# Two projections behind each layer norm computed from the stream before it is normalised

## The reference

```
x = layer_norm(ALPHA * x + mod[2] * y, ln1_g, ln1_b)          # y: the token mixer's output projection
f = conv_ffn(modulate(x, mod[3], mod[4]), w_up, ...)          # modulate(x, shift, scale) = layer_norm(x) * (1 + scale) + shift
x = layer_norm(ALPHA * x + mod[5] * f, ln2_g, ln2_b)
h = modulate(x, next_mod[0], next_mod[1]);  next_in = h @ w_in
```

## Time and profile before

| | us |
|---|---|
| median of 3 runs | 3637.96 |
| lowest and highest | 3637.43, 3638.48 |
| the profiled execution | 3641.97 |
| its span | 3639.8 |
| PE busy | 3432.4 |
| DVE busy | 1618.0 |
| POOL busy | 1076.3 |
| ACT busy | 1004.5 |

### The profile page before, as it was taken

One profiled execution on the slowest core, in us unless ns is written; L12 is line 12 of the kernel. 1 busy time (PEld: TensorE's weight loads), 2 busy tenths in 40 slices (PEclk: granted clock), 3 DMA queues, 4 the chain that ended last, 5 costly groups with the idle time before them and its releaser, 6 DMA issues.

```text
span 3639.8 us, 57152 instructions
## 1 busy us (share of the span) xinstructions
PE 3432.4 (94%) x24613; PEld 2827.6 (78%) x24613; DVE 1618.0 (44%) x2601; ACT 1004.5 (28%) x1438; POOL 1076.3 (30%) x412
## 2 busy tenths in 40 slices
PE   6999999979989999999999899999979899999998
PEld 5777778867768888888886677788867678888887
DVE  4333563056166334334334533463086564434436
ACT  4334564124132111111112333464133221111111
POOL 1212101302333333333333212201312444444443
PEclk9999999999999999999999999999989999999999
DMA  5111001352201111111112111000162111111111
GB/s 182 37 27 30 1 2 50 97 187 58 66 24 35 39 37 35 37 39 36 41 35 76 23 24 27 24 2 24 35 193 76 52 41 52 46 47 47 52 47 64
DMA packets 269678, 186.41 MB, mean 51 GB/s; under 512 B 45405, under 2 KB 249077, under 8 KB 269429
## 3 DMA queue, kind: packets, MB, share of 16 engines
q1 hardware_dynamic: 268272, 182.28, 16.7%
q10 hardware_dynamic: 1156, 0.48, 0.1%
HBM read 174.33 MB, written 8.39 MB: 50 GB/s over the span
## 4 chain that ended last, share of the span: by engine, by line
PE 83%; DVE 9%; issue 3%; ACT 2%; POOL 1%; DMA 1%; ACTq 0%; POOLq 0%; DVEq 0%; PEldq 0%
PE psum L1032 60%; PE psum L891 6%; PE psum L1132 5%; PE psum L1282 3%; PE psum L900 2%; PE psum L1210 2%; DVE f_t L2281 1%; PE psum L1058 1%; DVE y_chan L2172 1%; DVE c_x L2136 1%; PE psum L960 1%; PE psum L1241 1%; DVE h_lo L1931 1%; ACT f_t L2816 1%; PE psum L1366 1%
## 5 line engine op out<-in xcount | busy, mean ns | idle before, releaser
L1032 PE MATMUL psum<-h_hi,w_split 128*128 128x512 f32 (+1 forms) x5952 | 1437.7, 370 | 18.3 <-POOL w_split L846 8.1
L844 POOL TENSOR_SCALAR w_split<-w_raw 128x1024 fp32r<-128x1024 f32 x196 | 552.0, 2816 | 2390.4 <-PE psum L1032 1653.1
L1032 PEld LDWEIGHTS psum<-h_hi,w_split 128*128 128x128 f32 x5952 | 1030.3, 188 | 223.7 <-issue 12.0
L1032 PE MATMUL psum<-h_lo,w_split 128*128 128x512 f32 (+1 forms) x2976 | 799.9, 368 | 0.0
L1032 PEld LDWEIGHTS psum<-h_lo,w_split 128*128 128x128 f32 x2976 | 516.0, 188 | 97.6
L2281 DVE SCALAR_TENSOR_TENSOR f_t<-psum,vec,f_t 128x1023 f32<-128x1023 f32 (+1 forms) x264 | 260.2, 1013 | 705.4 <-ACT f_t L2816 702.3
L846 POOL TENSOR_TENSOR w_split<-w_raw,w_split 128x1024 fp32r<-128x1024 f32 x196 | 477.0, 2434 | 16.4
L1032 PE MATMUL psum<-f_hi,w_split 128*128 128x512 f32 (+1 forms) x1696 | 416.9, 371 | 15.7 <-DVE y_chan L2172 10.7
L2816 ACT ACTIVATE f_t<-psum,vec 128x1280 f32<-128x1280 f32 (+1 forms) x88 | 115.4, 1311 | 910.2 <-PE psum L1032 886.7
L1032 PEld LDWEIGHTS psum<-f_hi,w_split 128*128 128x128 f32 x1696 | 295.9, 188 | 80.3 <-issue 25.0
L2172 DVE SCALAR_TENSOR_TENSOR y_chan<-psum,mods,y_chan 128x1024 f32<-128x1024 f32 (+1 forms) x256 | 247.2, 1003 | 172.2 <-PE psum L1032 171.8
(11 more groups left out here) (275 smaller groups left out, 3471.6 us busy)
## 6 DMA issues: line engine op xcount, KB each, us to landing
w_raw<-in_w_up_dram SPq DMA_DIRECT2D x88, 512.0 KB, 3.8
ada_late<-in_w_ada_dram SPq DMA_DIRECT2D x32, 1024.0 KB, 7.3
w_raw<-in_w_down_dram SPq DMA_DIRECT2D x44, 512.0 KB, 3.8
w_raw<-in_w_in_dram SPq DMA_DIRECT2D x42, 512.0 KB, 3.9
ada<-in_w_ada_dram SPq DMA_DIRECT2D x4, 2048.0 KB, 17.9
ada_early<-in_w_ada_dram SPq DMA_DIRECT2D x8, 1024.0 KB, 5.3
x_first<-in_x_dram SPq DMA_DIRECT2D x8, 512.0 KB, 12.6
o_x<-in_x_dram SPq DMA_DIRECT2D x8, 512.0 KB, 3.9
```

Of the source, the lines that this page charges most:

```text
L844: pool.tensor_scalar(w_hi[:, n % 2], w_raw[:, n % 2], 1.0, None, ALU.mult).then_inc(s["w_hi_done"], 1)
L1032: last = pe.matmul(columns(key, t0, t0 + tn), weight, a[:, k, t0:t0 + tn], start=(k == order[0] and j == 0), stop=(k == order[-1] and j == 2))
```

## The change

For each stage, the two projections behind it no longer wait for the normalised halves.

- **Halves of the raw stream.** ACT writes `h_hi` = `y_chan` times the channel factor `ln_a` (`raw_high`), DVE writes the remainder to `h_lo` (`raw_low`). This happens as the channel tiles of the stream come, for stages 0 and 2 beside the last output projection. The two projections (`raw_gemms`) take these halves.
- **The tail within them.** The last statistics, the turning of the sums and a product of the small set-up rows with the raw, unsplit weights (`shift_products`, 16 matmuls of fp32) are issued between the steps `k` of the first projection. The spreading of the token factor and of the token rows, and the first corrections, are issued between those of the second. The spreading uses banks 6 and 7, piece by piece, and no accumulator slot.
- **Closing.** Three matmuls for each accumulator (`close`) add token rows times the shift vectors, behind step 3 of the second projection and at its end. DVE then multiplies the accumulator by the token factor: in place in phase F (`scaled`), on the way out in phase A (`raw_part`, which takes ACT's copies of `a_k` and `a_vt`).
- **The normed halves** are made afterwards into the same `h_hi`, `h_lo`, each `k` once the second raw projection has used it (`z_used`). The next projections, `up` 1 0 and `up` 1 1 with the second two steps behind, or `a_q` alone, run as they come.
- **DVE, ACT and POOL** get the work of FFN tile 0 (`scaled`, `conv`, `begin`, `silu`) between the steps of the normed halves, and POOL the splitting of the next weights between its products. The four residuals of the first pair stand together behind tile 1. The moments are spread within `up` 2 0.
- **Loads.** The weight loads that would overwrite the raw tiles' buffers wait for `raw_shift`.
- The barriers of all engines behind phases O and F of these stages become plain signals.

```diff
@@ load_weights
                     sp.wait_ge(s["w_ready"], n - 1)
+                    for st, raw in enumerate(RAW_TILES):
+                        if plan.tiles[n - 2] in raw:
+                            sp.wait_ge(s["raw_shift"], st + 1)
@@ POOL
-                pool.wait_ge(*freed("bc", st, 0))
-                for k in range(1, KT, 2):
+                pool.wait_ge(s["bc_taken"], done + many)
+                for n, k in enumerate(range(1, KT, 2)):
                     if k >= 3:
                         pool.wait_ge(s["hk_ready"], KT * st + k - 1)
-                    pool.tensor_tensor(kt_[:, 1, 0:w], y_chan[:, k, 0:w], r_b[:, 0:w], ALU.mult).then_inc(s["kt_ready"], 1)
+                    pool.tensor_tensor(kt_[:, 1, 0:w], y_chan[:, k, 0:w], r_of(st)[:, 0:w], ALU.mult).then_inc(s["kt_ready"], 1)
+                    if n < len(tiles):
+                        split_up_to(*tiles[n])
...
-                odd_products(2 * l)
+                odd_products(2 * l, [("up", l, 1, half) for half in range(2)])
@@ PE, raw_gemms
+                def shift_products():
+
+                    wait((s["set_widened"], st + 1))
+                    wait((s["set_taken"], 2 * st + 2))
+                    wait((s["var_ready"], 2 * st + 1))
...
+                        for k in range(KT):
+                            last = pe.matmul(psum[64 * t:64 * t + 56, 6, 3 * P:4 * P], set_wide[:, k, :], weight[:, k],
+                                             start=(k == 0), stop=(k == KT - 1))
+                    last.then_inc(s["raw_shift"], 1)
...
+                def close(t):
+                    wait((s["raw_shift_taken"], st + 1))
+                    wait((s["bc_taken"], done + 2 * many))
+                    for t0, tn, who in pieces(q_tiles(l)):
+                        rows_ = slice(64 * t + 32 * who, 64 * t + 32 * who + 24)
+                        last = pe.matmul(slot(*keys[t])[:, t0:t0 + tn], raw_vec[rows_, :], ranks_of(st)[rows_, t0:t0 + tn],
+                                         start=False, stop=True)
+                    fill(last, *keys[t])
...
+                gemm(tiles[0], keys[0], parts, ready=lambda k: (s["z_ready"], KT * st + k + 1),
+                     between={2: last_sums, 4: lambda: sum_columns(st), 6: shift_products}, fills=False, closes=False)
+                between = {n: spread_two(2 * n) for n in range(many)}
+                between.update({3: corrections(0, (0, 1)), 4: close_first, 5: corrections(1, (0, 1)), 6: corrections(1, (2,))})
+                gemm(tiles[1], keys[1], parts, between=between, used=s["z_used"], fills=False, closes=False)
+                close(1)
@@ PE, phase_a
-                    norm_tail(2 * l - 1)
-                    normed_gemms(2 * l - 1, [("in", l, COL["a_" + name]) for name in "kv"], [("A", l, r, name) for name in "kv"])
+                    raw_gemms(2 * l - 1, lambda: leave(pe, full("Y", l - 1, NPAIR - 1, KT - 1), "F", l - 1))
+                    normed_gemms(2 * l - 1, [("in", l, COL["a_q"])], [("A", l, r, "q")], groups(l), 0)
@@ PE, phase_f
-                normed_gemms(2 * l, [("up", l, 0, half) for half in range(2)], [("F", l, 0, half) for half in range(2)])
-                spread_moments(l)
+                raw_gemms(2 * l, lambda: leave(pe, full("W", l, KT - 1), "O", l))
+                normed_gemms(2 * l, [("up", l, 1, half) for half in range(2)], [("F", l, 1, half) for half in range(2)],
+                             groups(l), 2)
@@ DVE
+            def raw_low(st, k):
+
+                dve.wait_ge(s["z_hi"], KT * st + k + 1)
+                for a, b, who in [(0, LAT, 0)] + [(LAT, T, 1)] * (q_tiles(STAGES[st][0]) == NT):
+                    ins = dve.scalar_tensor_tensor(out=h_lo[:, k, a:b], in0=y_chan[:, k, a:b], scalar=ln_a[:, k, who:who + 1],
+                                                   in1=h_hi[:, k, a:b].bitcast(F32), op0=ALU.mult, op1=ALU.subtract)
...
+                normed_tiles(2 * l, {0: [partial(scaled, 0)], 1: [partial(conv, 0, 0), partial(scaled, 1)],
+                                     2: [partial(conv, 0, 1)]})
...
+                        for half in range(2):
+                            conv(f + 1, half)
+                        gated(f + 1)
+                        for k in range(4):
+                            residual(k)
```

More of the change, by code:

```diff
@@ L1012, in spread_gates, with gemm @@
                     last.then_inc(s["x1b_full"], 1)
-            def gemm(tile, key, parts, kt=KT, col=0, x_hi=h_hi, x_lo=h_lo, ready=None, between={}, order=None, fills=True):
+            def gemm(tile, key, parts, kt=KT, col=0, x_hi=h_hi, x_lo=h_lo, ready=None, between={}, order=None, fills=True,
+                     used=None, closes=True):
                 n = plan.tile[tile]
@@ new lines, in to @@
+                def to(part, many):
+                    return colmat[:, 0:n].rearrange("p c (r j) -> p c r j", j=32)[:, :, :, part:part + many]
+                dve.wait_ge(s["dve_step"], own.n)
+                for part in (0, 4):
+                    also(dve.tensor_copy(to(part, 3), four(high.bitcast(F32), 3)))
+                step(dve.tensor_tensor(to(8, 3), four(whole, 3), four(high.bitcast(F32), 3), ALU.subtract))
+                step(dve.tensor_copy(raw_high, raw))
+                for part in (12, 16):
+                    also(dve.tensor_copy(to(part, 4), four(raw_high.bitcast(F32), 4)))
@@ L2214, in phase_o @@
                     key = ("W", l, m)
+                    if m == KT - 1:
+                        for k in range(5):
+                            raw_low(2 * l, k)
                     dve.wait_ge(*full(*key))
@@ L2229, in phase_o @@
                         undo_residual(m + 2)
+                    if m == 2:
+                        widen_setup(2 * l)
+                for k in range(5, KT):
+                    last = raw_low(2 * l, k)
                 return last
@@ L2288, in conv, with scaled @@
                                 also(ins)
-                w = T if ctx_too else LAT
+                def scaled(half):
+                    acc = slot("F", l, 0, half)[:, 0:w]
+                    dve.wait_ge(*full("F", l, 0, half))
+                    say("scaled", dve.tensor_tensor(acc, acc, r_of(2 * l)[:, 0:w], ALU.mult))
                 def gated(f):
@@ L2516, in norm_tail, with raw_high @@
                         act.wait_ge(*corr_taken(st, k, piece))
+                    act.wait_ge(s["z_used"], KT * st + k + 1)
                     say("hk_hi", copy(h_hi[:, k, 0:w], kt_[:, k % 2, 0:w]))
+                    for work in behind.get(k, ()):
+                        work()
+            def raw_high(st, k, key):
+                l, which = STAGES[st]
+                act.wait_ge(s["set_built"], 2 * st + 2)
+                act.wait_ge(*freed(*key))
+                if not which and k < KT - 1:
+                    act.wait_ge(s["o_used"], (KT - 1) * l + k + 1)
+                for a, b, who in [(0, LAT, 0)] + [(LAT, T, 1)] * (q_tiles(l) == NT):
+                    ins = act.activation(h_hi[:, k, a:b], y_chan[:, k, a:b], ACT.Identity,
+                                         scale=ln_a[:, k, who:who + 1], bias=zeros[:, 0:1])
+                    if b == P * q_tiles(l):
+                        say("z_hi", ins)
+                    else:
+                        own.on(ins)
             def squares(st, m, key):
```

364 lines of the change are left out of this document (245 added, 119 removed).

## The result

The changed kernel takes 3648.77 us (median of 7 runs, 3644.38 to 3656.3), the kernel before 3637.96 (7 runs): a ratio of 1.0029, with a 95% interval of 1.0018 to 1.0039. So it is 10.8 us slower (6.5 to 14 by the interval), where 2.2 us less was forecast. The time lies just inside the stated range, whose upper end (3649) was set for the rival of the late start. The profiled execution took 3647.04, span 3645.2.

What follows compares the result with a forecast made beforehand. PE, busy 3432.4 of 3639.8 us, was taken as the bound, so only its waits or slow work could be won. Stage 0 +3.2, stage 2 +5.4, stage 1 -6.4: 2.2 us won, 3638.0 to 3635.8, range 3621 to 3649.

Steps and rivals of the forecast that it cites:

- the rival of the late start: Costlier fp32 matmuls and DVE's tail start the second raw projection 5 to 6 us later: 13.5 lost, 3651, chance 0.18.
- stage 0: First changed stage: fourth down projection at 1160.6 instead of 1163.8, a gain of 3.2 us.
- stage 1: Bias loads issued behind the eighth low half, 11.8 us later, delay the first scores: 6.4 us lost, 1.7 of it clock.
- stage 2: Like stage 0 with 1024 tokens: fourth down projection at 2976.1 instead of 2981.5, a gain of 5.4 us.
- the late residuals: DVE waits until 12 us into `up` 2 0, then does four residuals; PE waits 1.4 at `up` 3 0, 0.9 later.
- the widening: Widening of sets on DVE, taken to cost nothing beside projections; 1.5 us a stage if that cover is gone.
- PE's raw part: First raw projection with statistics, turning and 16 fp32 matmuls (4.0 us): 21.5 us in stages 0 and 1, 17.3 in stage 2.
- B: Time in each stage when the last output or down projection ends and the last statistics start, before the change; 998.7 in stage 0.
- Stage 0's chain: DVE, POOL and ACT make normed halves in turn; eighth low half at T + 58 = 1078.2, DVE the bound.
- T: Start of the second raw projection, forecast at B + 21.5 in stages 0 and 1, about B + 17.3 in stage 2.
- The rival of a quick chain: Pairs of normed halves take 9.4 us in all stages, fp32 matmuls 2.0: 13 won, 3625, chance 0.27.
- The clock rival: PE stays at 1.2 GHz in the normed steps, costing stages 0 and 2 2 to 3 us each: 3641, chance 0.12.

Runs made afterwards that it cites:

- bias_early: Changed kernel, with SP issuing the 16 bias loads behind stage 1's fourth low half instead of its eighth: 3641.78 us, 1.0005 of the kernel before.
- before_bias_early: Kernel before the change, with the same earlier issue of the bias loads: 1.0006 of the kernel before.
- widen_later: Changed kernel, with stage 1's widening moved from ahead of the last down pair's first sum to behind its third: 3643.98 us, 1.0013 of the kernel before.
- moments_ahead: Changed kernel, with the moments' first pieces spread in the normed pair's last two steps, the next two ahead of `up` 2 0: 3638.1 us, 1.0006 of the kernel before.
- all_three: Changed kernel with the edits of bias_early, widen_later and moments_ahead together: 3625.24 us, 0.9959 of the kernel before.
- all_warm: all_three, plus the eighth tile's residual ahead of the fourth tile's second-half taps, and 18 unread matmuls behind stage 1: 3613.67 us, 0.9931 of the kernel before.

## Why the prediction was wrong

Against the forecast, stage 0 is 6.8 us worse, the loop 2.2, stage 1 0.4 and stage 2 6.0. The step that failed is the price of the late residuals, and next to it the widening that was taken as hidden.

**Right.** PE's raw part: the second raw projection started at B + 20.9 in stages 0 and 1 and B + 17.0 in stage 2 (21.5 and 17.3 forecast), with the fp32 products at 3.31 (4.0 taken, between 2.0 and 6.8). Stage 0's chain: eighth low half at T + 58.4 (58.0). Stage 1: loses 6.8 (6.4), for the reason given, as bias_early and before_bias_early show. The eighth low half came at T + 51.1 (49.1), the first scores 16.8 behind it (17.5), and the clock cost 1.4 (33.8 against 32.4 for the round; 1.7 forecast). That the sum comes out within 0.4 is partly luck: these errors offset each other, and the code of before alone swings from 116.5 to 120.8 there. The rival of a quick chain is refuted by the same rows. The late start, whose 3651 is near the result, had the sum right and the cause wrong: T was 0.6 earlier than forecast, not 5 late. The clock rival named the normed steps. The clock did fall there (0.72 between B + 50 and B + 60), and in widen_later, where it was at 0.50, this cost 2.0 us, the size that the rival named for one stage. In the changed kernel's own execution the eighth low half of stage 0 came as forecast, so its loss there lies elsewhere (below).

**Wrong: the residuals (6 us in stage 0, most of 6 in stage 2).** The step said that DVE "waits until 12 us into `up` 2 0, then does four residuals (12 + 1.6 beside POOL)", that `up` 3 0 waits 1.4 for them and a down projection 0.9. The mechanism was there and its size wasn't: the waits were 2.71, 2.03 and 3.87, 8.6 instead of 2.3. With the 1.5 of the clock below, less the 1.1 by which `up` 2 0 came early, that is the loss of stage 0. It gave the collision 1.6 us for one block, where five operations over three splittings lost 7.4, and it counted the 12 us of waiting as free, since PE was busy meanwhile. It wasn't free, because DVE still had the residuals to do before the first sum. With the moments ahead, DVE starts them 4.6 us earlier and PE gets 6.2 back. That the forecast's 1160.6 (B + 161.9) nearly appears in moments_ahead (B + 160.96) shows that the rest of the working held for stage 0. In stage 2 the fourth down projection came 6.9 later than forecast, and moments_ahead gives 4.8 of it back. There the eighth low half came 4 us later besides (T + 47 against T + 43); why isn't shown.

The Trainium skill (GPSIMD Engine Reference, Specifications) has GpSimd's SBUF interfaces shared with VectorE, with contention for instructions with two SBUF inputs. The trace agrees: 1.49 becomes 2.32 to 3.70 beside splitting (except where DVE's operation began first), and the taps, with one input in PSUM, stay at 3.38.

**Wrong: the widening (2.1 us).** The prediction counted at nothing "squares, sets and widening, which lie in DVE's idle time beside projections". That holds in stages 0 and 2, where it stands behind the third sum. For stage 1 the code puts it behind `before_tail`, that is behind the last sum of the pair before the last, and just ahead of the last pair's first sum. The price named for a lost cover (1.5 us a stage) was right in size, only the place wasn't looked at.

**Missed: a clock drop behind a wait (1.5 us).** The matmuls behind the fourth down projection's wait took 2.34 instead of 1.33. The length of the wait alone doesn't decide it: in the earlier trace rows a wait of 2.56 had no such rows behind it (17.7 us to the mark instead of 19.2), while moments_ahead and all_three, with the same 2.56, had them (19.2). The Trainium skill (TensorE: Matmul & The Clock Gate, What's actually happening) says that activity releases the throttle; all_warm agrees for the round behind stage 1 (0.95 to 1.00 with 18 idle matmuls).

## What to carry to other kernels

Time that is won on the critical engine has to be followed through the helper engine's queue up to the next point where the two meet. If work that used to lie in the stage (here the moments and the residuals) now comes later, its start time counts, even where the critical engine is busy meanwhile. A step that releases a DMA must be followed to that DMA: stage 1, the best of the three in the end, first lost 6.8 us to a load that waited for more than the memory it overwrites. And before two kernels are compared by one trace each, it helps to look at how far a stretch with unchanged code swings between them. An operation with two SBUF inputs should be timed against the other engine's schedule before it is moved.

## What the runs showed that was not expected

- DVE's wait of 5.34 us for the moments pushed its block into POOL's splittings: 7.4 us of excess in five operations, 1.5 when the block started 4.6 us earlier.
- The same code took up to 2.0 us more in stage 0 and up to 4.3 us more in stage 1, with the granted clock at 0.50 for longer.
- 16 fp32 products with 56 weight columns and 128 streamed ones take 3.31 us together, and 16 more of them 2.73, 0.17 us each. Doubling (1.85 for eight) would give 3.7.
- After the edits stage 1 took 111.1 instead of the 117.2 of before, and 1.1 of this goes with matmuls that nobody reads.
